# Prompt attention of a hybrid decoder step: which engine multiplies the probability rows by their reciprocal sums

## The reference

```python
def block(args):
    i, qlb, qrb = args
    s = (jnp.einsum('bqhr,bkr->bhqk', qlb, c_kv)
         + jnp.einsum('bqhp,bkp->bhqk', qrb, k_r)).astype(jnp.float32)
    qpos = i * Q_BLOCK + jnp.arange(Q_BLOCK)
    s = jnp.where(kpos[None, :] <= qpos[:, None], s, -jnp.inf)
    p = jax.nn.softmax(s, axis=-1).astype(c_kv.dtype)
    return jnp.einsum('bhqk,bkr->bqhr', p, c_kv)
```

## Time and profile before

| | |
|---|---|
| median of 3 runs | 1304.1 us (1303.97 to 1307.81) |
| the profiled execution's own time | 1302.94 us |
| its span, first to last instruction | 1301.2 us |
| PE busy | 1259.5 us (97%) |
| DVE busy | 910.2 us (70%) |
| ACT busy | 593.2 us (46%) |
| POOL busy | 577.7 us (44%) |

### The profile page before, as it was taken

One profiled execution on the slowest core, in us unless ns is written; L12 is line 12 of the kernel. 1 busy time (PEld: TensorE's weight loads), 2 busy tenths in 40 slices (PEclk: granted clock), 3 DMA queues, 4 the chain that ended last, 5 costly groups with the idle time before them and its releaser, 6 DMA issues.

```text
span 1301.2 us, 24156 instructions
## 1 busy us (share of the span) xinstructions
PE 1259.5 (97%) x9110; PEld 1184.4 (91%) x9110; DVE 910.2 (70%) x1462; ACT 593.2 (46%) x1222; POOL 577.7 (44%) x575
## 2 busy tenths in 40 slices
PE   9999999999999989998999999999999999999987
PEld 7878998888786569998999999999999999999987
DVE  5983167776766436278955786676676679889986
ACT  7433235666665343124354544455444444444452
POOL 1732344354431227652465977788877800000030
PEclk9999999999999999999999999999999999999998
DMA  9420102000027535630221222212212497867403
GB/s 331 135 62 33 49 5 76 5 21 1 18 69 274 195 151 181 194 101 21 84 83 59 92 83 76 91 60 91 96 67 88 145 340 252 301 198 257 146 1 138
DMA packets 70405, 151.93 MB, mean 117 GB/s; under 512 B 9138, under 2 KB 16690, under 8 KB 69842
## 3 DMA queue, kind: packets, MB, share of 16 engines
q1 hardware_dynamic: 70290, 150.39, 34.4%
HBM read 127.80 MB, written 22.56 MB: 116 GB/s over the span
## 4 chain that ended last, share of the span: by engine, by line
PE 75%; DVE 13%; issue 4%; ACT 3%; DMA 2%; POOL 2%; SPq 1%; DVEq 0%; POOLq 0%; ACTq 0%
PE ps L1206 22%; PE ps L1208 21%; PE ps L1207 21%; PE ps L1452 2%; DMA araw<-in_w_dn 1%; PE ps L1510 1%; PE ps L1464 1%; PE ps L1572 1%; DVE vf L2578 1%; PE ps L1465 1%; ACT pTH L1890 1%; DVE nmx L2729 1%; SPq L733 1%; DVE x L2487 1%; DVE hL L2525 1%
## 5 line engine op out<-in xcount | busy, mean ns | idle before, releaser
L1161 POOL TENSOR_TENSOR chunk<-wraw,chunk 128x256 fp32r<-128x256 f32 x193 | 164.0, 873 | 60.7 <-ACT chunk L1890 60.5
L1206 PE MATMUL ps<-bHL,aHL 128*128 128x272 f32 x616 | 179.0, 291 | 5.4 <-DVE bHL L3273 5.1
L1208 PE MATMUL ps<-bHL,aHL 128*128 128x272 f32 x616 | 178.0, 289 | 0.0
L1207 PE MATMUL ps<-bHL,aHL 128*128 128x272 f32 x616 | 177.8, 289 | 0.0
L1161 POOL TENSOR_TENSOR chunk<-wsum,chunk 128x256 fp32r<-128x256 f32 x134 | 115.0, 876 | 27.6 <-ACT chunk L1890 27.4
L1890 ACT ACTIVATE chunk<-wraw 128x256 fp32r<-128x256 f32 x193 | 74.9, 412 | 105.0 <-PE ps L1208 48.5
L1206 PEld LDWEIGHTS ps<-bHL,aHL 128*128 128x128 f32 x616 | 116.7, 189 | 6.5 <-DVE bHL L3273 6.2
L1207 PEld LDWEIGHTS ps<-bHL,aHL 128*128 128x128 f32 x616 | 116.7, 189 | 0.0
L1208 PEld LDWEIGHTS ps<-bHL,aHL 128*128 128x128 f32 x616 | 116.6, 189 | 0.0
L1187 POOL TENSOR_TENSOR sqy<-sqy 128x1088 f32<-128x1088 f32 (+1 forms) x2 | 4.2, 2122 | 202.0 <-ACT sqy L2452 201.9
L1098 POOL TENSOR_TENSOR prob<-prob,rsm 128x128 f32<-128x128 f32 (+5 forms) x48 | 49.6, 1042 | 78.2 <-DVE rsm L2718 78.2
(11 more groups left out here) (497 smaller groups left out, 4632.8 us busy)
## 6 DMA issues: line engine op xcount, KB each, us to landing
araw<-in_w_dn SPq DMA_DIRECT2D x121, 256.0 KB, 3.2
wraw<-in_w_gu SPq DMA_DIRECT2D x44, 512.0 KB, 3.8
cp<-in_cache SPq DMA_DIRECT2D x64, 272.0 KB, 4.6
ab<-acts SPq DMA_DIRECT2D x34, 272.0 KB, 4.1
raw<-in_w_out SPq DMA_DIRECT2D x16, 512.0 KB, 4.3
acts<-bufC SPq DMA_DIRECT2D x22, 272.0 KB, 2.1
xt<-in_x_tok SPq DMA_DIRECT2D x9, 512.0 KB, 5.6
x<-x2s SPq DMA_DIRECT2D x8, 544.0 KB, 5.8
```

What stands on the lines that cost most here:

```text
L1161: pool.tensor_tensor(x[:, 1, :], source_of(i, step), x[:, 0, :], ALU.subtract).then_inc(cw_lo, 1)
L1206: nc.tensor.matmul(out, wh, xh, start=start, stop=False, skip_group_check=onto)
L1207: nc.tensor.matmul(out, wh, xl, start=False, stop=False, skip_group_check=onto)
L1208: return nc.tensor.matmul(out, wl, xh, start=False, stop=stop, skip_group_check=onto)
```

## The change

GpSimd's `normalise` and its calls go. VectorE multiplies each row right behind its reciprocal. The semaphore `s_pn` of the GpSimd multiplications goes, and `s_pd` counts all four rows of a unit. Nothing is moved between the other instructions.

```diff
-            def normalise(u):
-                for qi in range(3):
-                    r, qt = 4 * u + qi, 4 * (u % 2) + qi
-                    n = P * (qt + 1)
-                    row = prob[:, prob_at(qt):prob_at(qt) + n]
-                    pool.wait_ge(s_rc, r + 1)
-                    pool.tensor_tensor(row, row, rsm[:, r % 4:r % 4 + 1].broadcast_to((P, n)),
-                                       ALU.mult).then_inc(s_pn, 1)
...
             head_pieces(1)
-            normalise(0)
             for u in range(UNITS):
                 p = u // 4
                 if u % 4 == 3 and u < UNITS - 1:
                     query_lo(p + 1)
-                if u < UNITS - 1:
-                    normalise(u + 1)
...
-                        if kt == 0 and qi < 3:
-                            pe.wait_ge(s_pn, 3 * u + qi + 1)
-                        elif kt == 0:
-                            pe.wait_ge(s_pd, u + 1)
+                        if kt == 0:
+                            pe.wait_ge(s_pd, 4 * u + qi + 1)
...
-                if u and qi < 3:
-                    dve.wait_ge(s_pn, 3 * (u - 1) + qi + 1)
-                elif u:
-                    dve.wait_ge(s_pd, u)
+                if u:
+                    dve.wait_ge(s_pd, r - 3)
                 nc.vector.reciprocal(rsm[:, s], sm[:, s]).then_inc(s_rc, 1)
-                if qi == 3:
-                    qt = 4 * (u % 2) + 3
-                    row = prob[:, prob_at(qt):prob_at(qt + 1)]
-                    dve.wait_ge(s_rc, r + 1)
-                    nc.vector.tensor_scalar(row, row, rsm[:, s], None, ALU.mult).then_inc(s_pd, 1)
+                qt = 4 * (u % 2) + qi
+                row = prob[:, prob_at(qt):prob_at(qt + 1)]
+                dve.wait_ge(s_rc, r + 1)
+                nc.vector.tensor_scalar(row, row, rsm[:, s], None, ALU.mult).then_inc(s_pd, 1)
...
-            dve.wait_ge(s_pn, 3 * UNITS)
-            dve.wait_ge(s_pd, UNITS)
+            dve.wait_ge(s_pd, 4 * UNITS)
```

More of the change, by code:

```diff
@@ L506, in build @@
         o_low = sem("o_low")
-        s_ready, s_nm, s_exp, s_rc, s_pn, s_pd = (
-            sem("s_" + n) for n in ("ready", "nm", "exp", "rc", "pn", "pd"))
+        s_ready, s_nm, s_exp, s_rc, s_pd = (
+            sem("s_" + n) for n in ("ready", "nm", "exp", "rc", "pd"))
         t_ready, t_hi, t_free, pv_x, o_free = (sem(n) for n in ("t_ready", "t_hi", "t_free", "pv_x", "o_free"))
```

## The result

| | before | after |
|---|---|---|
| median | 1305.15 us (1303.97 to 1307.81, 4 runs) | 1325.23 us (1323.93 to 1328.76, 4 runs) |
| profiled execution, its span | 1302.94, 1301.2 us | 1325.29, 1323.6 us |
| mean granted TensorE clock | 0.992 | 0.977 |
| VectorE, GpSimd busy | 910.2, 577.7 us | 931.2, 528.2 us |

The ratio is 1.0148 [1.0131, 1.0165]: slower, as forecast, but by 20.1 us where 13.4 were forecast. The two profiled executions are 22.35 us apart: that of the kernel before was its fastest here. GpSimd lost its 49.6 us and VectorE got 21.0.

What follows compares the result with a forecast made beforehand. TensorE's products wait for `pTL` on VectorE, whose list order counts; GpSimd's multiplication is off the path. Terms summed to 13.4 us, on the profiled 1302.94 giving 1316.3, plus 1.16 for the median: 1317.5 us, range 1310 to 1322 (own range 1314 to 1320).

Steps and rivals of the forecast that it cites:

- start: Start of the attention: row 0's multiplication waits for GpSimd's L972, 0.5 us left after slack, bounds 0 and 1.4.
- unit 0: First unit, which lacks the addition: 0.6 us more, taken from between 0.55 and 1.22.
- even units: Seven even units, long rows added: the last `pTL` comes 1.22 us later in each, 8.5 us in all.
- u % 4 of 1: Odd units with short rows added, partly covered by waits for ScalarE: 0.25 us each, 4 times, 1.0 us.
- units 3 and 7: VectorE's second multiplication is blocked by GpSimd's L972, so `pTL` 7 comes 1.35 us later in each: 2.7 us.
- unit 11: No weight tile behind its queries; waits for ScalarE take nearly all of the added work: 0.1 us.
- Rival A: Units 3 and 7: VectorE stays blocked through both L969 and L972; + 2.7 us, 1320.2 us, chance 0.13.
- B: Even units: delays don't add up, only the last multiplication shows, 0.505 us in each; 8.4 us, 1312.5, chance 0.13.
- C: Even units: `pTL` 3 is not what holds the last product, so no slower; 1303.4 us, chance 0.05.
- D: VectorE falls behind for good, an odd unit's delay joining the next unit's; some 9 us more, 1326, chance 0.05.

Runs made afterwards that it cites:

- short_rows: The changed kernel with the long rows (640, 768, 896 keys) given back to GpSimd; VectorE multiplies the short ones and row 3: 1308.79 us, 1.0027.
- long_rows: The changed kernel with the short rows (128, 256, 384 keys) given back to GpSimd; VectorE multiplies the long ones and row 3: 1318.67 us, 1.0110.
- late_multiply: The changed kernel with all multiplications on VectorE, but placed behind the `pTL`s that TensorE waits for; row 3's reciprocal also later where u % 4 is 1: 1304.39 us, 0.9988.
- late_multiply_2: late_multiply with the first unit's multiplications moved later too: 1304.54 us, 0.9992 against the kernel before.
- idle_tensor: The kernel before, with one added TensorE wait ahead of each even unit's last product, for the maximum of row 3: 1319.90 us, 1.0104.
- keep_clock: The changed kernel with 9 (unit 0: 5) unread TensorE multiplications of ones ahead of each even unit's last product: 1321.82 us, 1.0130.
- keep_clock_2: keep_clock with fewer multiplications of ones: 2 in unit 0, 5 where u % 4 is 0, 4 where it is 2: 1320.28 us, 1.0105.
- clock_and_split: The changed kernel with the multiplications of ones of keep_clock_2 and the GpSimd wait of hold_split: 1317.25 us, 1.0082.
- hold_split: The changed kernel, with GpSimd's weight split in units 3 and 7 held until VectorE has multiplied row 3: 1321.77 us, 1.0118.

## Why the prediction was wrong

**What held.** The direction, and the mechanical terms near enough. Its parts against the landmarks, forecast first: start 0.5 and 0.38; unit 0 0.6 and 0.64; even units 8.5 and 8.15; u % 4 of 1 1.0 and 0.5; units 3 and 7 2.7 and 2.4; unit 11 0.1 and 0.02. 13.4 and 12.1 us. With these alone the profiled execution would have taken 1315 us. For unit 10 the working gave 1.22 and it was 1.0: the last `pTL` came 1.03 later after the first reciprocal. 0.12 of the shortfall is slack that I overlooked between the addition and row 2's reciprocal (355.24 to 355.96 is 0.72, 369.70 to 370.30 is 0.60), the rest is some 0.02 in each of three steps. Where u % 4 is 0 it was 1.34 to 1.39, more than 1.22: there `pTL` 3 began only 0.19 after row 2's reciprocal before the change (281.12 to 281.31 in unit 4), not 0.30, and the 0.12 of slack is missing too. So one unit stood for two kinds, and that 8.15 comes so near to 8.5 is in part luck. `short_rows`, `long_rows` and `late_multiply` show these terms apart.

**Which side wins the port.** The forecast had the first multiplication of unit 3 slip in between L969 and L972 and the second blocked. VectorE in the changed kernel, against the earlier trace rows:

```profile
269.64 0.56 DVE L2706 TENSOR_SCALAR prob<-prob,rsm 128x128 f32<-128x128 f32 x1
...
271.23 1.51 DVE L2706 TENSOR_SCALAR prob<-prob,rsm 128x256 f32<-128x256 f32 x1
...
272.66 0.41 DVE L2729 TENSOR_TENSOR pTL<-ps,pTH 128x256 fp32r<-128x256 f32 x1
```

And GpSimd, against the earlier trace rows:

```profile
269.07 1.05 POOL L969 TENSOR_SCALAR w0H<-raw 128x1024 fp32r<-128x1024 f32 x1
270.20 2.39 POOL L972 TENSOR_TENSOR w0L<-raw,w0H 128x1024 fp32r<-128x1024 f32 x1
```

The first began under L969 and ended at 270.20, when L972 began; the second began under L972 and ended just behind it (272.74 against 272.59). That is the forecast's picture, with 1.51 where it said about 1.6. Rival A, blocked through both, fell. The Trainium skill, SBUF — State Buffer, section "SBUF: two separate sides", calls the port that the two share an exclusive lock, held for a whole instruction; the rows agree, and add that VectorE got it between two of GpSimd's instructions. Only the multiplications were held: under L972 a `pTL` (270.11, 0.55 us) and a maximum (270.58, 0.54 us) took what they take elsewhere. At the start, the multiplication took 1.80 us, to the end of L972:

```profile
217.47 1.80 DVE L2706 TENSOR_SCALAR prob<-prob,rsm 128x128 f32<-128x128 f32 x1
```

**What failed.** The last sentences on the even units: the last product waits for `pTL` "with nothing else in TensorE's list before it", and what is behind moves along, "so the delay is neither doubled nor won back". They priced TensorE's wait as time alone and took every TensorE duration at the speed of the trace before, though behind such waits the speed changed. The forecast has no term and no rival for the clock. With waits of 1.46 us it fell three times in the attention (6.8 us) and stayed down longer in the sample queries (3.1 us): 10 us beside the 12.1 of the sum. Only the 6.8 are shown to come of the change: `late_multiply_2`, without these waits, spent 22.43 us in the last interval of its profiled execution, as much as the change's 22.47. `idle_tensor` shows that the clock can fall behind such a wait alone. In `keep_clock`, `keep_clock_2` and `clock_and_split`, which fill the wait, none of nine places has the fall. `clock_and_split` shows that what is left is near the mechanical sum. The Trainium skill, TensorE: Matmul & The Clock Gate, section "A second HAM failure mode: psum-queue depth-cycling", says of another kernel that short and frequent idle times between groups of matmuls make the clock swing between its two levels, and gives no price for one. The windows above agree in part: 0.50 to 0.55 was granted, but behind one wait of 1.46 us each time.

**Whether it could have been seen.** The kernel before ran at a mean of 0.992 and had one stretch at 0.51, in the sample queries (416 to 419 us), right behind the stage that the change makes wait. That was in its trace, and I did not weigh it.

**The rivals.** A fell, as shown above. B (8.4 us, 1312.5: only the last multiplication shows) fell: the even intervals grew by 1.0 to 1.4, not 0.5. C fell: the last products waited 1.08 and 1.46 us. D named a time near the one measured (1326), for another reason: VectorE's delay did not join that of the next unit, odd intervals grew by 0.13 where the clock held. That a number is met does not show its mechanism.

**What stays open.** What decides where the clock falls. In the change, `long_rows` and `hold_split` nine waits of 1.46 us stand in units 4, 8 and 12, and eight were followed by a fall, not that of unit 4 in `long_rows`. None of the nine of 1.08 us in units 2, 6 and 10 was, and of seven of 1.24 us in `idle_tensor`, units 0 to 12, one. The eight profiles in which no wait for `pTL` in the attention is over 0.85 us have one fall there, in `keep_clock_2`. The length of the wait is not all that differs: behind units 4, 8 and 12 TensorE goes on with matmuls of 128 columns, behind 2, 6 and 10 with matmuls of 512, and no run separates the two.

Nor is it shown what decides how long the clock stays down in the sample queries. It falls there in all twelve profiles. In the kernel before it fell at about 415.5 us with no TensorE wait of 0.2 us or more since 401.6, so a wait is not needed. In the change it came down right behind unit 14's wait of 1.08 us and stayed down for 10 us; the last interval is 19.3 us in four kernels, 20.9 to 22.5 in seven and 25.22 in `idle_tensor`.

## What to carry to other kernels

An engine at 70% has no room where its list is in the order of need: price an added instruction by what stands behind it in that list, and put it behind the instruction that another engine waits for. `late_multiply` did the same work as the change and lost nothing. Where the edit lengthens TensorE's waits, look at the granted clock of every stretch, put the clock in as a term and as a rival of its own, and let the range reach there: here it was 6.8 of 22 us, or 10 with the sample queries.

## What was not expected of the hardware

- In the attention TensorE's clock fell to half (0.50) behind single waits of 1.24 to 1.46 us, and stayed there 3 to 10 us, with TensorE busy all that time.
- The same kernel part fell at one place in one execution and not in the next kernel's (13.24 us behind unit 5 in the change, 9.86 in `long_rows`, both with 13.57 to 13.60 before it).
- A multiplication of VectorE that waited for GpSimd's instruction got in before GpSimd's next one, although GpSimd's gap was 0.08 us (0.56 us in all). The forecast had this as the likelier of two cases.
